# Two transformer blocks on one core: the modulation units of the first block's FFNs stand behind up-projections 1, 2, 4 and 5 of each seven instead of 0, 2, 3 and 5

## What is computed

```
def channel_mixer(h, w_up, ffn_dw_w, ffn_dw_b, w_down):
    u = causal_depthwise_conv(h @ w_up, ffn_dw_w, ffn_dw_b)
    a, b = jnp.split(u, 2, axis=-1)
    return (jax.nn.silu(a) * b) @ w_down

x = x + g2 * channel_mixer(modulate(rms_norm(x, ffn_norm_g[l]), sh2, sc2), ...)
mod = silu(c) @ w_mod[l] + b_mod[l]        # six vectors of 1024 a layer; nine in the second block
```

## Time and profile before

| | us |
|---|---|
| median of three runs | 2813.73 |
| lowest, highest | 2807.42, 2815.07 |
| the profiled execution | 2805.84 |
| its span, first to last instruction | 2803.9 |
| up-projections of the first layer's FFN | 390.3 to 535.6 |
| up-projections of the second layer's FFN | 961.6 to 1107.3 |
| granted TensorE clock, mean | 0.994 |

### The profile page before, as it was taken

The page is one execution under the profiler, slowest core; times in us unless marked ns, Lnnn a source line. Parts: engine busy times, 40 slices in busy tenths (PEclk is TensorE's granted clock), DMA queues, the critical chain, the costliest instruction groups (busy, mean ns, idle before and its releaser), DMA issues.

```text
span 2803.9 us, 38041 instructions
## 1 busy us (share of the span) xinstructions
PE 2714.6 (97%) x15414; PEld 2258.5 (81%) x15414; DVE 1735.7 (62%) x2457; ACT 1134.4 (40%) x1718; POOL 181.5 (6%) x132
## 2 busy tenths in 40 slices
PE   7989999999989999999999999999999999999998
PEld 5778889977778889777878787888877788878996
DVE  5798467656995677654546446555574455375654
ACT  3546356635554466422222333222232222345442
POOL 0071000000520000100000000000010000100000
PEclk9999999999999999999999999999999999999999
DMA  8542457646523576454454212443335543221453
GB/s 337 202 154 83 139 196 245 230 163 218 172 82 116 198 255 237 143 187 181 158 186 158 84 61 98 143 150 135 135 121 183 192 150 136 97 98 54 168 186 105
DMA packets 121885, 444.08 MB, mean 158 GB/s; under 512 B 13424, under 2 KB 14832, under 8 KB 121328
## 3 DMA queue, kind: packets, MB, share of 16 engines
q1 hardware_dynamic: 121712, 441.66, 45.2%
HBM read 440.56 MB, written 1.05 MB: 157 GB/s over the span
## 4 chain that ended last, share of the span: by engine, by line
PE 85%; DVE 11%; ACT 2%; issue 1%; DMA 1%; SPq 0%; DVEq 0%; ACTq 0%
PE ps L627 22%; PE ps L628 21%; PE ps L629 21%; PE ps L631 14%; PE ps L624 5%; DVE rests L1697 3%; PE ps L625 2%; DVE area L1806 2%; DVE rs L1758 1%; DMA ring<-stream 1%; DVE area L1768 0%; DVE x_sb L1794 0%; ACT L1336 0%; ACT L1520 0%; DVE rt L1821 0%
## 5 line engine op out<-in xcount | busy, mean ns | idle before, releaser
L627 PE MATMUL ps<-h_split,heads 128*128 128x256 f32 (+1 forms) x3048 | 1013.0, 332 | 26.4 <-DVE rests L1697 17.2
L628 PE MATMUL ps<-h_split,heads 128*128 128x256 f32 (+1 forms) x3048 | 990.9, 325 | 0.0
L629 PE MATMUL ps<-h_split,rests 128*128 128x256 f32 (+1 forms) x3048 | 990.8, 325 | 0.0
L1274 ACT ACTIVATE heads<-ring 128x1024 fp32r<-128x1024 f32 x548 | 564.4, 1055 | 503.8 <-PE ps L629 207.7
L1697 DVE TENSOR_TENSOR rests<-ring,heads 128x1024 fp32r<-128x1024 f32 x548 | 686.7, 1278 | 125.1 <-ACT heads L1274 117.2
L627 PEld LDWEIGHTS ps<-h_split,heads 128*128 128x128 f32 x3048 | 583.1, 191 | 126.0 <-DVE h_split L1778 16.6
L628 PEld LDWEIGHTS ps<-h_split,heads 128*128 128x128 f32 x3048 | 583.4, 191 | 50.3 <-issue 5.3
L629 PEld LDWEIGHTS ps<-h_split,rests 128*128 128x128 f32 x3048 | 583.1, 191 | 46.7
L1930 DVE TENSOR_TENSOR sg<-sg,ps 128x512 f32<-128x512 f32 (+1 forms) x88 | 54.7, 622 | 300.8 <-PE ps L629 249.5
L627 PE MATMUL ps<-hid_split,heads 128*128 128x512 f32 (+1 forms) x594 | 225.3, 379 | 2.0 <-DVE rests L1697 1.8
L1430 ACT ACTIVATE sg<-ps 128x512 f32<-128x512 f32 (+1 forms) x88 | 47.7, 542 | 440.4 <-PE ps L629 440.4
(11 more groups left out here) (201 smaller groups left out, 2913.2 us busy)
## 6 DMA issues: line engine op xcount, KB each, us to landing
ring<-stream SPq DMA_DIRECT2D x830, 512.0 KB, 3.4
consts<-constants SPq DMA_DIRECT2D x1, 1728.0 KB, 10.8
x_sb<-x_in SPq DMA_DIRECT2D x1, 1024.0 KB, 10.7
x_sb<-ctx_in SPq DMA_DIRECT2D x1, 1024.0 KB, 4.8
out<-area SPq DMA_DIRECT2D x1, 1024.0 KB, 4.8
consts<-constants SPq DMA_DIRECT2D x1, 576.0 KB, 8.3
cols<-columns SPq DMA_DIRECT2D x1, 538.0 KB, 9.5
cols<-columns SPq DMA_DIRECT2D x1, 157.5 KB, 2.3
```

The costliest lines, as they stand in the source:

```text
L627: nc.tensor.matmul(out, lhsT[0], rhs[0], start=first, stop=False)
L628: nc.tensor.matmul(out, lhsT[0], rhs[1], start=False, stop=False)
L629: ins = nc.tensor.matmul(out, lhsT[1], rhs[0], start=False, stop=last)
L1274: nc.scalar.activation(heads[:, n % HEADS_RING, :], ring[:, u % RING, :], ACT.Copy)\
```

## The change

```
-SPREAD_UNITS = {0: [0, 1], 2: [2, 3], 3: [4, 5], 5: [6, 7], SPREAD: []}
+SPREAD_UNITS = {1: [0, 1], 2: [2, 3], 4: [4, 5], 5: [6, 7], SPREAD: []}
```

## The result

The changed kernel takes 2819.08 us (median of 13 runs, 2814.59 to 2821.22) against 2813.00 for the kernel before in 13 runs beside it. The ratio is 1.0021, 95% interval [1.0012, 1.0031]: 6.1 us slower, inside the 0.3% taken as no change, and inside the forecast range. The forecast's middle was +4.1 us; rival 2 (+5.8) is the nearest case.

A forecast was written before the change was run, and what follows sets the result against it. PE, busy 97% of the span, was taken as the bound. Two uncovered guest places and one clock fall, +1.18 + 1.18 + 1.7 = +4.1 us on 2813.73, gave 2817.8 us, range 2808 to 2823.

The forecast's parts named there:

- rival 2: Granted clock falls behind both longer waits before pair 4, one per layer: +5.8 us, 2819.5 us; chance 0.20.
- Place 3 to 4: Guests moved from behind pair 3 to behind pair 4 no longer cover PE's wait: +1.18 us in each layer.
- The chain behind the landing: Late weight unit for pair 3, then ACT and DVE work, sets pair 4's start; claimed unchanged by the move.
- The clock: Behind the two longer PE waits at pair 4, one fall of the granted clock expected: +1.7 us, bounds 0 and 3.4.
- The sum: All terms over both layers: +1.18 + 1.18 + 1.7 = +4.1 us, giving 2817.8 us.
- Places 7 to 8, 10 to 11, 14 to 15, 17 to 18: Guest moves in the later groups: ACT and DVE keep up with PE, 0.8 us or more left; cost 0.
- the five close places: Two guest places with one pair between, at 4/5, 8/9, 11/12, 15/16, 18/19: DMA queue keeps up; cost 0.
- The reserve: At the close guest places, 3.3 us left before a late weight landing would stop PE.
- The limit of about 358 GB/s: A core's share of HBM; the close places ask 302 GB/s, below it, which would also make their cost 0.
- Place 0 to 1: Guests moved from behind pair 0 to behind pair 1, both layers: one step on PE, nothing moves, cost 0.

The follow-up runs named there:

- e4: Changed kernel plus two idle products of constants on PE ahead of pair 4 in both layers; 2814.90 us, ratio 1.0013 to the kernel before.
- e3: Kernel before with four guest units behind pair 3 and none behind pair 5 in the first group; 2811.37 us, ratio 1.0000.
- e6: Kernel before with first-group guests moved: two units behind pair 1, four behind 4, two behind 5; 2818.06 us, ratio 1.0028.
- e2: Kernel before with the new places only in the two later groups, first group kept; 2811.99 us, ratio 1.0002.
- e5: Kernel before with first-group guests moved: none behind pair 0, two units behind 2, four behind 3, two behind 5; 2808.06 us, ratio 0.9990.
- e8: Kernel before with first-group guests moved to two units each behind pairs 2, 3, 4 and 5; 2811.06 us, ratio 1.0001.
- e1: Kernel before with the new places only in the first group of both layers; 2819.38 us, ratio 1.0028.

## Why the prediction was right, and where its size was off

**Place 3 to 4: right.** It was priced at +1.18 us a layer, with idle times of 2.47 and 2.81. The first layer showed 2.54. The guests came 7.41 us behind pair 4's start and not the forecast 5.8, as the clock had fallen. The layers of e4, where no clock falls, showed +1.30 and +1.13, of which 0.17 and 0.02 are the landing.

**The chain behind the landing: right, but not as fixed as I took it.** I took the landing and the chain behind it to stay. In the first layer it did, 16.49 for 16.42 us. In the second it came 0.86 us later (2.65 for 1.79), and went through to PE. The prediction put this term at nothing, on the ground that all up to pair 3 is in the same order. That the order is the cause is not shown: over the executions above, orders that are the same up to pair 3 gave 1.64 to 2.65 there, and e3, whose guests up to pair 3's are those of the kernel before and more of them follow, gave 2.63. What makes this one landing vary stays open. Nor is the landing all of the chain: with no late landing for pair 3, e6 still waited 2.09 us. ACT's table load of 1.28 us stands in that chain too, and no run takes it out.

**The clock: the mis-sized term.** The step "I take one half for each of the two longer waits, so one fall, +1.7 us" measured two falls at 1.5 us, 3.0. The half came from six waits at other places, three of them with a fall. At this place all waits of 2.20 us and more, filled or not, had a fall (2.20, 2.54, 2.54, 2.59, 3.55, 3.67) and none up to 2.09 had one (the longest 2.02, 2.09, 2.09). Elsewhere the old odds still hold: a wait of 2.22 us before 725.25 had no fall in one execution and one of 2.23 had a fall in another, and 3.02 us before 861.86 had none. In e6 it fell behind a wait of 0.87 us and stayed behind one of 0.99 at the same matmuls. So the length of the wait alone does not decide, and why this place falls each time isn't settled. That the filled kernel is 4 us faster in the medians too fits falls in most executions, not in the profiled ones alone; only the profiled ones show them.
The sentence that the prediction quotes from the Trainium skill, "TensorE: Matmul & The Clock Gate", Part 1, that the default state is throttled, does not say behind which wait the clock falls; the prediction took it for every gap, which made two falls. At this place the trace agrees with that reading, two of two; for the kernel's other waits only in part, as before.

**The sum.** Forecast 2.4 + 1.7 = 4.1. Measured 2.4 for the places, 3.0 for two falls, 0.9 for the late landings (0.07 and 0.86): 6.3 in the stages, 6.1 in the medians. Rival 2's +5.8 lies nearer partly by luck: it took 3.4 us for two falls, which is 0.4 too much, and nothing for the landings, which is 0.9 too little.

**Places 7 to 8, 10 to 11, 14 to 15, 17 to 18, and the five close places: right.** e2 gives 1.0002 [0.9993, 1.0010], and the stages' +0.16 and +0.19 are the landing in front of pair 3. ACT's waits for landings grew from 3.3 and 3.6 us to 7.4 and 10.2 in the changed kernel, and PE did not feel those at the moved places. The reserve has an end. With 3.3 us beyond ACT's wait of 1.89 it was forecast where ACT waits 5.2 us; in e6 PE waited 0.42 us for the rests where ACT had waited 5.13, and not at all for them where it had waited 4.29, but the copy of the rows had less room.
The limit of about 358 GB/s that the prediction took from the Trainium skill, "DMA: Bandwidth & Descriptors", Specifications, decides nothing here. The queue moved 393 GB/s over 4.4 us in e6.

**Place 0 to 1: right**, as pair 4 starts at the same distance in the first layer.

**What stays open.** For e5 to e8 the medians all lie above the stages: -1.9 against -3.2, +8.1 against +4.9, +2.3 against -0.1, +1.1 against -1.1. These four share one set of executions of the kernel before, whose median is 2809.98. Its other sets have 2813.00, 2812.53 and 2812.59. Against 2812.6 the four would stand at -4.5, +5.5, -0.3 and -1.5 us, close to the stages. So the gap lies for the most part in what they were compared with; why that set is lower stays open. The intervals are about 2.4 us to each side, and the stages of every kernel come from one execution each.

## What to carry to other kernels

Work that an engine does in front of a wait whose end it doesn't set is free up to the length of the wait; moved behind it, it costs its whole time, so first ask what ends the wait, and then what stands in front. On TensorE price a longer wait twice, once for the work that it no longer covers and once for the clock behind it, and try a few idle matmuls in it before the order is given up: here two in each layer were worth about 3 us. The better order here (e5) did both things at once, with the late unit earlier in the stream and the guests right ahead of the wait; a table like this one should be chosen by its first group, for the others had room.

## What the runs showed of the hardware that I had not expected

- Added matmuls make it faster: with two idle products, 1.8 us of a 2.6 to 2.8 us wait, the clock stayed at 1.00, and the median went from 2819.38 us (e1, the same first group) to 2814.90 (e4).
- Behind the same matmul, of like executions, the granted clock fell after 2.23 us of idle time and stayed at 1.00 after 2.22; at pair 4 it fell six times out of six from 2.20 to 3.67 us, and each fall cost 1.4 to 1.5 us. Behind the matmuls of the rows in e6 it fell after 0.87 us and stayed after 0.99.
- One landing of 0.52 MB, in the same order of the queue, came 1.64 to 2.65 us late for ACT in the second layer, but only 1.45 to 1.62 in the first.
